# Gated DeltaNet scan: who computes the log-decay, decay, update and attention matrices

## What is computed

```python
cum = jnp.cumsum(g, axis=-1)
decay = jnp.exp(jnp.where(incl, cum[..., :, None] - cum[..., None, :], -jnp.inf))
kk = jnp.einsum('nbhid,nbhjd->nbhij', k, k)
t_mat = jnp.where(strict, beta[..., :, None] * kk * decay, 0.0) + jnp.eye(c, dtype=F32)
rhs = jnp.concatenate([k * (beta * jnp.exp(cum))[..., None], v * beta[..., None]], -1)
sol = lax.linalg.triangular_solve(t_mat, rhs, left_side=True, lower=True, unit_diagonal=True)
qk = jnp.einsum('nbhid,nbhjd->nbhij', q, k) * decay
def step(s, inp):
    v_new = uc - jnp.einsum('bhck,bhkv->bhcv', wc, s)
    s_next = s * gl[..., None, None] + jnp.einsum('bhck,bhcv->bhkv', kt, v_new)
    o = jnp.einsum('bhck,bhkv->bhcv', qd, s) + jnp.einsum('bhcj,bhjv->bhcv', qkc, v_new)
```

## Time and profile before

| | |
|---|---|
| median of three runs | 2843.75 us |
| the profiled execution | 2838.83 us, its span 2837.0 us |
| PE busy | 2669.6 us (94%) |
| DVE busy | 1600.2 us (56%) |
| ACT busy | 954.7 us (34%) |
| POOL busy | 561.7 us (20%), 232 instructions |
| mean granted TensorE clock | 0.973 |
| scan of layer 0 | about 277 to 524 us of the span |
| scan of layer 1 | about 1820 to 2051 us |

### The profile page before, as it was taken

The page is one execution under the profiler, slowest core; times in us unless marked ns, Lnnn a source line. Parts: engine busy times, 40 slices in busy tenths (PEclk is TensorE's granted clock), DMA queues, the critical chain, the costliest instruction groups (busy, mean ns, idle before and its releaser), DMA issues.

```text
span 2837.0 us, 49791 instructions
## 1 busy us (share of the span) xinstructions
PE 2669.6 (94%) x21046; PEld 2123.6 (75%) x21046; DVE 1600.2 (56%) x2848; ACT 954.7 (34%) x1502; POOL 561.7 (20%) x232
## 2 busy tenths in 40 slices
PE   7899999899999999999999989898899999999998
PEld 1388778788888888887787538777778787888676
DVE  4745676527554443435747754667637754352856
ACT  0334323322222343224532234443243333432542
POOL 0022000120113212321023512200031132242032
PEclk9999989999999999999999999999899999999999
DMA  8421000232222112220034551100053231231133
GB/s 252 155 69 43 18 26 20 100 123 97 79 87 88 60 53 99 88 82 27 30 119 146 203 191 60 46 25 25 25 178 119 97 109 59 86 127 63 34 119 111
DMA packets 95164, 250.94 MB, mean 88 GB/s; under 512 B 11010, under 2 KB 28804, under 8 KB 94432
## 3 DMA queue, kind: packets, MB, share of 16 engines
q1 hardware_dynamic: 84170, 219.56, 23.0%
q10 hardware_dynamic: 10774, 28.19, 2.9%
HBM read 205.12 MB, written 35.26 MB: 85 GB/s over the span
## 4 chain that ended last, share of the span: by engine, by line
PE 73%; DVE 16%; ACT 4%; issue 3%; DMA 3%; ACTq 1%; SPq 0%; DVEq 0%
PE ps L995 18%; PE ps L996 17%; PE ps L997 17%; PE ps L1565 4%; PE ps L1003 3%; PE ps L1592 2%; PE ps L1012 2%; DVE t_gcv L2254 1%; PE ps L1135 1%; PE ps L1024 1%; PE ps L1575 1%; DVE t_grp L2254 1%; PE ps L1589 1%; PE ps L1181 1%; DVE t_grp L2608 1%
## 5 line engine op out<-in xcount | busy, mean ns | idle before, releaser
L956 POOL TENSOR_TENSOR t_wlo<-t_raw,t_whi 128x1024 fp32r<-128x1024 f32 x217 | 535.0, 2467 | 2201.8 <-ACT t_whi L1698 2201.8
L995 PE MATMUL ps<-t_u_hi,t_whi 128*128 128x512 f32 (+1 forms) x2368 | 868.9, 367 | 16.7 <-ACT t_oT L1769 3.6
L996 PE MATMUL ps<-t_u_lo,t_whi 128*128 128x512 f32 (+1 forms) x2368 | 838.3, 354 | 0.0
L997 PE MATMUL ps<-t_u_hi,t_wlo 128*128 128x512 f32 (+1 forms) x2368 | 834.2, 352 | 0.0
L995 PEld LDWEIGHTS ps<-t_u_hi,t_whi 128*128 128x128 f32 x2368 | 452.6, 191 | 91.1 <-issue 19.7
L1698 ACT ACTIVATE t_whi<-t_raw 128x1024 fp32r<-128x1024 f32 x235 | 248.2, 1057 | 800.5 <-PE ps L997 693.9
L997 PEld LDWEIGHTS ps<-t_u_hi,t_wlo 128*128 128x128 f32 x2368 | 450.9, 190 | 64.3
L996 PEld LDWEIGHTS ps<-t_u_lo,t_whi 128*128 128x128 f32 x2368 | 453.2, 191 | 57.3 <-issue 3.0
L2881 DVE TENSOR_REDUCE t_amx<-ps 128x1 f32<-128x768 f32 (+1 forms) x120 | 101.5, 846 | 151.2 <-PE ps L1565 150.6
L1769 ACT ACTIVATE t_grp<-ps 128x256 f32<-128x256 f32 (+2 forms) x192 | 80.0, 436 | 275.1 <-PE ps L1012 160.5
L995 PE MATMUL ps<-t_b_hi,t_whi 128*128 128x512 f32 (+1 forms) x384 | 139.0, 362 | 6.7 <-DVE t_b_lo L2246 3.4
(11 more groups left out here) (305 smaller groups left out, 3829.9 us busy)
## 6 DMA issues: line engine op xcount, KB each, us to landing
t_raw<-in_w_in SPq DMA_DIRECT2D x184, 512.0 KB, 3.5
t_raw<-in_w_ada SPq DMA_DIRECT2D x48, 512.0 KB, 4.6
t_raw<-in_w_br SPq DMA_DIRECT2D x32, 512.0 KB, 4.0
t_raw<-in_w_out SPq DMA_DIRECT2D x24, 512.0 KB, 4.3
t_sg<-gate_logits SPq DMA_DIRECT2D x28, 384.0 KB, 4.7
hs<-t_hstage ACTq DMA_DIRECT2D x20, 512.0 KB, 3.6
t_hring<-hs SPq DMA_DIRECT2D x20, 512.0 KB, 6.1
t_prob<-t_pT ACTq DMA_DIRECT2D x56, 128.0 KB, 2.1
```

Of the source, the lines that this page charges most:

```text
L956: pool.tensor_tensor(lo, raw[:, s % RAW, :], hi.bitcast(f32), ALU.subtract)\
L995: pe.matmul(o, lh, rh, start=first, stop=False)
L996: pe.matmul(o, lh, rl, start=False, stop=False)
L997: return pe.matmul(o, ll, rh, start=False, stop=last)
```

## The change

The beta factor and the causal mask are multiplied once into the decay matrix, on GpSimd. Update matrix and attention matrix then need one 128x512 operation per direction on DVE. The update matrix is made one level later (after level 5's merges) and waits for GpSimd ("g_dm") in place of ACT ("g_ed"). The log decays are made on ACT, one direction at level 1 and one at level 2, and k_tail is split over levels 3 and 4. At the start of a scan ACT makes round 0's log decays between `identities(0)` and the exponentials. GpSimd's `factors(l, t)` stands in its list ahead of the low part of the tile after the one that PE is at when the decays of round t are made.

```diff
+        def factors_at():
+            for l in range(DEPTH):
+                first = CONV_OF[STREAM.index((l, "w", O_GDN + P * 11))] + 1
+                tiles_in = scan_tiles(l) - LAST_TILES - first_tiles(l)
+                for t in range(NT):
+                    n = steps_by(l, SCAN_PHASES // NT * (t - 1) + 5, SCAN_PHASES, tiles_in) // gate_units(l) if t else 0
+                    yield l, t, first + first_tiles(l) + n + 1
...
         @block.gpsimd
         def _(pool):
+            done = [0]
+            def factors(l, t):
+                for d in range(2):
+                    i0 = chunk(t, d) * 8 + d * 4
+                    done[0] += 1
+                    pool.wait_ge(sems["g_ed"], done[0])
+                    for h in range(HEADS):
+                        x = grp[:, d, 1, h * P:(h + 1) * P]
+                        last = pool.tensor_scalar(x, x, gsc[:, 0, i0 + h:i0 + h + 1], None, ALU.mult)
+                    last.then_inc(sems["g_db"], 1)
+                    pool.wait_ge(sems["g_db"], done[0])
+                    x = by_head(grp[:, d, 1, :])
+                    pool.tensor_tensor(x, x, over_heads(cst[:, C_GE if d else C_LE, :]), ALU.mult)\
+                        .then_inc(sems["g_dm"], 1)
             for c, s in enumerate(CONV_AT):
                 if c in IN_CHAIN:
                     continue
+                for l, t in FACTORS_AT.get(c, ()):
+                    factors(l, t)
...
+                def log_decays(t, d):
+                    c = chunk(t, d)
+                    for h in range(HEADS):
+                        i = c * 8 + d * 4 + h
+                        last = run(scan_m(t, d)[:, h * P:(h + 1) * P], cst[:, C_GE if d else C_LE, :], ACT.Copy,
+                                   scale=gs[:, 9, i:i + 1])
+                    ln.done(last, "g_gm")
                 identities(0)
+                for d in range(2):
+                    log_decays(0, d)
                 decays()
...
-                        if lv == 4 and t + 1 < NT:
-                            k_tail(t)
+                        if t + 1 < NT:
+                            if lv < 3:
+                                log_decays(t + 1, lv - 1)
+                            if lv in (3, 4):
+                                k_tail(t, lv - 3)
...
                 def m_of(t):
                     for d in range(2):
-                        i0 = chunk(t, d) * 8 + d * 4
-                        ln.take("g_ed")
+                        ln.take("g_dm")
                         ln.take("g_kk")
-                        ln.step(each(lambda h, s: stt(scan_m(t, d)[:, s], ps[:, 3 * d, s],
-                                                      gsc[:, 1, i0 + h:i0 + h + 1], grp[:, d, 1, s],
-                                                      ALU.mult, ALU.mult)), "g_m")
+                        ln.step(stt(scan_m(t, d), ps[:, 3 * d, :], -1.0, grp[:, d, 1, :], ALU.mult, ALU.mult), "g_m")
...
-                                    step(each(lambda h, s: stt(grp[:, d, 6, s], ps[:, B, s],
-                                                               gsc[:, 0, i0 + h:i0 + h + 1],
-                                                               grp[:, d, 1, s], ALU.mult, ALU.mult)))
-                                    a = by_head(grp[:, d, 6, :])
-                                    ln.done(tt(a, a, over_heads(cst[:, C_GE if d else C_LE, :]), ALU.mult), "g_a")
-                        if lv == 2 and t + 1 < NT:
-                            for d in range(2):
-                                log_decays(t + 1, d)
-                        if lv == 4 and t + 1 < NT:
+                                    ln.done(tt(grp[:, d, 6, :], ps[:, B, :], grp[:, d, 1, :], ALU.mult), "g_a")
+                        if lv == LEVELS - 2 and t + 1 < NT:
                             m_of(t + 1)
```

More of the change, by code:

```diff
@@ L361, in trunk @@
                  "cum_ps", "cum_exp",
-                 "g_gm", "g_d", "g_ed", "g_kk", "g_qk", "g_m", "g_a",
+                 "g_gm", "g_d", "g_ed", "g_dm", "g_db", "g_kk", "g_qk", "g_m", "g_a",
                  "g_q", "g_q_ok", "g_p", "g_pt", "g_x", "g_y", "g_yf", "g_ktail", "g_ks", "g_r", "g_vn", "g_vn_ok", "g_pre",
@@ L708, in halves_by @@
             return 2 * p if p < 2 else 4 + (p - 2) * (2 * n * len(segs(l == 0)) - 4) // (phases - 4)
+        def factors_at():
[5 more added lines that the diff above has]
+                    yield l, t, first + first_tiles(l) + n + 1
+        FACTORS_AT = {}
+        for l, t, c in factors_at():
+            FACTORS_AT.setdefault(c, []).append((l, t))
         block = es.enter_context(nc.Block())
@@ L957, in _ @@
                     .then_inc(sems["w_ready"], 1)
-                l = STREAM[s][0]
-                if l == 0 and STREAM[s + 1][0] != l:
+                if STREAM[s][0] == 0 and STREAM[s + 1][0] != 0:
                     for i in range(NT):
@@ L1939, in by_rows, with k_tail @@
                     ln.done(last, name)
-                def k_tail(t):
-                    for d in range(2):
-                        c = chunk(t, d)
-                        by_rows(ktail[:, d, :], ktok[:, c, :],
-                                lambda h: ec[:, 2 * d + 1, c * 8 + d * 4 + h:c * 8 + d * 4 + h + 1], "g_ktail")
+                def k_tail(t, d):
+                    c = chunk(t, d)
+                    by_rows(ktail[:, d, :], ktok[:, c, :],
+                            lambda h: ec[:, 2 * d + 1, c * 8 + d * 4 + h:c * 8 + d * 4 + h + 1], "g_ktail")
+                def log_decays(t, d):
+                    c = chunk(t, d)
+                    for h in range(HEADS):
[3 more added lines that the diff above has]
+                    ln.done(last, "g_gm")
                 identities(0)
+                for d in range(2):
+                    log_decays(0, d)
                 decays()
@@ L2515, in gdn_project @@
                     if j == 10:
-                        step(ts(gsc[:, 1, :], gsc[:, 0, :], -1.0, None, ALU.mult))
                         dve.wait_ge(sems["cum_exp"], l + 1)
@@ L2533, in gdn_scan @@
             def gdn_scan(l):
[L2534 to L2542, removed]
                 def each(f):
@@ L2588, in within_chunk @@
                                                       gtok[:, c, s], ALU.mult, ALU.add)), "g_o2")
-                for d in range(2):
-                    log_decays(0, d)
                 fence(ln, "dve")
```

2 lines of the change are left out of this document (removed).

## The result

The changed kernel took 2815.51 us, the median of five runs (2807.85 to 2819.11), against 2839.12 us (2830.51 to 2845.26) for the kernel before in the same measurement: a ratio of 0.9917, 95% interval 0.9888 to 0.9945. A second measurement (twelve runs of after, 23 of before) gave 2823.31 against 2830.03 us, 0.9971 (0.9957 to 0.9985). The two intervals don't meet. The profiled execution took 2815.93 us, its span is 2814.0 us, 23.0 less than before.

The account below looks back on a forecast made before the run. PE, busy 94%, was taken to stall behind DVE's attention matrix, with its clock halved afterwards. From 2838.8 us, -31.5 for stalls, +11.7 for starts and +5.3 for the tile gave 2824.3, forecast 2824 us, range 2808 to 2852.

Parts of the forecast that it names:

- Faster: Outcome case for the whole kernel: a time under 2829.5 us, given a chance of 0.48.
- The stall behind the attention matrix: Level 2 of the scans' rounds: PE's wait for DVE's predicated copy goes, saving 19.5 us in layer 0, 12 in layer 1.
- Rival D: Rounds hardly move: their excess is not from the stall, only idle time of 13.5 and 8.2 us counts; 2834 us, 10%.
- no 0.50 clock in the rounds' middle: Sign in the profile after: TensorE no longer drops to half its clock behind level 2's stall; 1.2 us charged per stall.
- Log decays on ScalarE, update matrix later: In the rounds, eight copies on ACT and an update matrix one level later were to cost nothing.
- rival B: PE's level 3 wait or q_of behind ACT's new copies takes half of DVE's gain; 2840 us, 20%.
- F: GpSimd's time per direction for the beta and mask multiplies, put at 3.1 us; the sum moves 6 us per us.
- The start: Start of each scan: uncovered log decays and GpSimd work delay it by 2F - 0.35, 5.85 us per layer, 11.7 in all.
- The tile: Layer 0, low part queued behind round 5's factors: 2F - 2.1 late, 4.1 us, plus 1.2 of clock, 5.3 us.
- DVE against GpSimd: Slowdown of DVE operations running beside GpSimd's in the scans: charged nothing.
- Rival A: GpSimd slow from fixed cost: past F = 5.5 the update matrix is late in ten rounds, 26 us per us; 13%.

Follow-up runs that it names:

- second pair: The kernel before and the changed kernel, both unchanged, traced once more: 2837.16 us (one run) and 2823.31 us (median, 0.9971 of before).
- heavy_pointer: Changed kernel, but DVE makes each attention matrix in five operations of the old kinds, scalar read from SBUF: 2842.39 us, 1.0044 of before.
- logs_on_dve: Changed kernel, but DVE makes all log decays again, round 0's at the start, the others at level 2: 2814.48 us, 0.9943 of before.
- broadcast_beta: Changed kernel, but GpSimd multiplies beta in with one broadcast 128x512 operation per direction in place of four 128x128 ones: 2813.51 us, 0.9936 of before.
- tile_first: Changed kernel, but GpSimd makes the next tile's low part ahead of the factors in all rounds but the first: 2816.39 us, 0.9944 of before.
- slow_gpsimd: Changed kernel, but GpSimd multiplies by the causal mask three times in each direction: 2853.71 us, 1.0082 of before.
- heavy_attention: Changed kernel, but DVE makes each attention matrix in five operations, the scalar an immediate 1.0: 2837.98 us, 1.0017 of before.

## Why the prediction was right, and where it was not

The forecast was 2824 us, the range 2808 to 2852; measured was 2815.51, and 2823.31 in the second measurement. "Faster" was the likeliest case; the first measurement is there (2815.5 under 2829.5), the second, at 0.29%, is within the 0.5%. The ledger of the profiled executions tells more: the sum had -31.5 + 11.7 + 5.3 = -14.5 us for the scans, and they changed by -12.0 (second pair: -12.9). That this is near is partly luck, since the terms were off in both directions: the gain was larger than forecast (34.8 us in place of 31.5) and so were the costs (16.1 in place of 11.7 at the starts, some 6.7 in place of 5.3 at the tile). The first measurement stands 8.5 us under the forecast because of the 11 us outside the scans. The effect in the scans, some 12 to 13 of 2835 us or 0.4 to 0.5%, lies at the border of what counted as faster.

- **The stall behind the attention matrix, -31.5: right as a whole, its two parts mis-sized.** Layer 0's rounds fell by 12.3 us with the tile in them. With 5.5 measured and the forecast's 1.2 for its clock, which no run shows apart, that is 19.0 without (forecast 19.5). Layer 1's fell by 15.8 (forecast 12). The second pair gives 15.3 + 6.7 and 13.6. PE's waits fell to 1.3 and 1.9 us (under 3 forecast), the four intervals from k_by_k to k_by_k in layer 0 are 35.7, 36.1, 36.4 and 36.7 us (37 forecast; 42, 40, 43 and 39 before). Of the 31.5 us the prediction had some 22 as idle time and 9.7 as clock, 1.2 for each of eight stalls. Measured are 16.9 us of idle time and 16.7 us of shorter products (15.6 and 19.0 in the second pair). So a stall's clock cost about twice what was charged, and the idle time came out smaller; the two errors hide each other. Layer 1 shows it best: its clock is 0.99 in the rounds where it was 0.93. Rival D, by which only the idle time counts, falls. The sign "no 0.50 clock in the rounds' middle" held but for the tile's stall and for round 5 (497 to 503 us).
- **What the stall consists of: two thirds the attention matrix.** Of the gross gain of 19.0 + 15.8 = 34.8 us heavy_pointer takes back 23 to 25. The remaining 10 stay gained with the attention matrix as heavy as before, so they go to the rest of the change: round 1's stall is 1.07 us in heavy_pointer and was 3.18 before, beside a low part. With the light attention matrix the log decays cost nothing on DVE (logs_on_dve), so the parts don't add up one by one. No run has the light attention matrix alone; that the two thirds are its own share is argued from heavy_pointer.
- **Log decays on ScalarE, update matrix later, nothing: right for the rounds.** They are the same either way, and rival B (q_of behind ScalarE's new copies, half of the gain lost) falls.
- **F: mis-sized.** It is 3.66 us, forecast 3.1. The four small multiplies take 2.34 us and not 1.6, the masked one 1.28 (forecast 1.3), and the handovers some 0.05 (forecast 0.2). The nearest row for a fixed cost was a memset of one column, 0.098 us, and the multiplies have more of it. The Trainium skill, "GPSIMD Engine Reference", section 3.1 (its figure is for an add), gave an estimate of 3.7 for F, and the trace has 3.66. Its parts are less well borne out: it left 0.28 us fixed in every instruction, and broadcast_beta leaves some 0.46 by the estimate above. By it the change of the scans was -10.9 us.
- **The start: mis-sized, 8.05 us per layer where 5.85 was forecast.** 2F - 0.35 is 7.0 with the measured F. The missing 1.1 is a term that the sum did not have: PE now waits 4.61 us for ScalarE's log decays, the clock falls to 0.50, and the decays' product takes 3.78 us where it took 1.95 us. With the log decays back on DVE it takes 1.96 us, and the start 11.87 us.
- **The tile: right in place and cause, its stall mis-sized with F.** 2F - 2.1 = 5.2 with the measured F; 5.53 us are measured where 4.1 was forecast, at the place that was named and with the clock at 0.50 behind it. The 1.2 us for that clock are not shown apart: without the stall tile_first's products are 4.1 to 4.6 us shorter, with the second fall of the clock in it.
- **DVE against GpSimd, nothing: right for this change**, since at the start its four predicated copies from SBUF meet no low part (1.81 us). tile_first moves one there, and they take 3.15 us.
- **Rival A: its mechanism is real, and GpSimd is not that slow.** The deadline was put at F = 5.5. At F = 6.3 the prediction's 26 us per us gives 0.8 x 26 = 21 beyond the deadline; with (5.5 - 3.7) x 6 = 11 up to it, 32. slow_gpsimd has 35 to 37. The sum fits, made up otherwise: DVE waits in nine rounds, but PE for over 1 us in four only, and layer 1's tile, which the prediction gave room up to F = 5.3, stalls by 2.70 us.

## What to carry to other kernels

A stall costs its idle time and, where the clock falls behind it, longer products. Here the second part was as large as the first: 16.7 us beside 16.9 in the rounds, and from heavy_attention to heavy_pointer 10.2 beside 2.4. So what the last 0.5 us of a stall are worth has to be measured. When work is moved to an engine with slack, ask where that slack has no cover: the start of a phase that nothing runs beside, and a shared list in which something urgent stands behind it. And compare stretches between landmarks: of the 23 us that the first two profiles differ by, 11 lay outside the scans, where next to nothing was changed.

## What was not expected of the hardware

- Behind the same idle of 1.46 us TensorE's clock fell to 0.50 in one round of heavy_attention and stayed at 1.00 in another.
- From heavy_attention to heavy_pointer PE was idle 2.4 us more in the rounds, and the same products took 10.2 us more.
- DVE's 128x128 multiply of two tensors and a scalar took 282 ns on average with the scalar as an immediate (heavy_attention) and 344 ns with a scalar of each partition (heavy_pointer).
- GpSimd's 128x512 multiply took 1039 ns with beta broadcast along the row and 1273 ns with the mask, which is 128 elements repeated four times.
- A stretch of identical code of some 1300 us between the scans varied from 1294.6 to 1307.1 us; the clock fell at different places in it.
